# Local attention in a two-block fp32 kernel: GpSimd forms the high half of the gated output itself

## The chip, the cores and the metric

The kernel runs on one core of a Trainium2 chip. The metric is the device time of one execution in microseconds; lower is better. Engines are named as in the profile: PE (TensorE), DVE (VectorE), ACT (ScalarE), POOL (GpSimd), SP (SyncE, which issues DMAs here).

## The reference

Two transformer blocks over 512 tokens of width 1024, all in fp32. The part of the second block that matters here:

```python
q = rope(sw_q ...); k = rope(sw_k ...)
o_sw = sliding_window_sink_attention(q, k, sw_v, attn_sinks[l], valid)   # 16 query heads, 2 KV heads,
                                                                         # window 128, softmax with a sink
y_sb = (o_sb * jax.nn.silu(sb_z)) @ w_branch_sb[l]
y_sw = (o_sw * jax.nn.silu(sw_z)) @ w_branch_swa[l]                      # gate, then a 1024 x 1024 product
merged = jax.nn.sigmoid(g_sb) * y_sb + jax.nn.sigmoid(g_sw) * y_sw
h = h + merged @ w_out[l]
```

## The kernel before

Every fp32 matrix product is made of three PE passes. Each operand is split into a high part, rounded to the type fp32r that PE takes, and a low part, the remainder `value - high`, and PE adds high·high, low·high and high·low. So whatever feeds a product has to be split on the way.

The local attention works in 16 windows, `w = 4 n + u`: block `n` of 128 queries, and `u` one of four groups of four heads. Each engine runs its own instruction list, written by hand, and the lists meet in semaphores. For window `w`:

- PE: `window_scores` into PSUM; DVE: `window_max` (L1752) and `window_bias` (L1761, L1762, four numbers per partition); ACT: `window_exp` (L1081); DVE: `window_norm` (L1777 sum, L1778 reciprocal, which raises `inv_ready`).
- POOL: two products of the probabilities by the inverse sums (L619), each 128x512.
- PE: transposes (L2322); ACT copies them out of PSUM as the high part `pwt` (L905), DVE makes the low part (L1526); PE: `window_values` (L2336, L2338).
- ACT: `other_half` copies one half of the result (`other_part`, L905), DVE adds the other (`window_out`, L1743) into `yw`, a tile with two buffers, and raises `swo_read`.
- The gate: POOL multiplies `yw` by `gate_sw` in place (`window_gated`, L602), ACT copies the product to its place in `qw` as fp32r, the high part (`window_out_hi`, L905), and POOL subtracts that from `yw` and writes the low part beside it (`window_out_lo`, L610), which raises `ysw_ready`.

`qw` feeds the product with `w_branch_swa` after the last window; its first matmul waits for `ysw_ready` 16. `window_out(w)` on DVE waits for `ysw_ready` of window `w - 2`, since it writes the same buffer of `yw`.

The lists are skewed. In its turn `w` POOL makes the two L619 of window `w`, the gate product of window `w - 2` and the low part of window `w - 3`; DVE makes the norm of `w`, `window_out(w - 2)`, the low part of `pwt` of `w - 1`, and maximum and bias of `w + 2`; ACT makes the high part of `pwt` of `w - 1`, the exponentials of `w + 1`, `window_out_hi(w - 3)` and `other_half(w - 1)`. PE fills its list with single steps (three matmuls each) of the merge gate's product, one per turn and two in turns 4, 8 and 12. In turns 10 and 11 DVE also splits a quarter each of a weight slab (L1526, `wlo<-raw,whi`, 128x512). Turns are named by this `w`; a turn of POOL is counted from the start of its first L619.

Of the kernel before, what the change touches and what calls it, by code (L numbers as in the profile page):

```python
# [5 lines left out]
F32 = mybir.dt.float32  # L6
F32R = mybir.dt.float32r
ALU = mybir.AluOpType
# [4 lines left out]
P = 128  # L13
# [66 lines left out]
def insert_dim(ap, pos, n, step=0):  # L80

    dims = [list(d) for d in ap.ap]
    dims.insert(pos, [step, n])
    return bass.AP(ap.tensor, ap.offset, dims)
# [7 lines left out]
def build(nc, a, out):  # L92
    with ExitStack() as ctx:
        names = {}

        def sem(name):
            names[name] = ctx.enter_context(nc.semaphore(name))
            return names[name]
# [3 lines left out]
        def sb(name, shape, dt=F32, offset=None):  # L102
            size = 4 * int(np.prod(shape[1:]))
            size = (size + 31) // 32 * 32
            if offset is None:
                offset = at[0]
                at[0] += size
                assert at[0] <= nc.sbuf_usable_end, (name, at[0], nc.sbuf_usable_end)
            t = nc.alloc_sbuf_tensor_at(name, shape, dt, offset=offset)
            return t  # L110
# [94 lines left out]
        qw = sb("qw", [P, 16, SEQ], F32R)  # L205
# [7 lines left out]
        gate_sw = sb("gate_sw", [P, 8, SEQ])  # L213
        tokm = sb("tokm", [META, 3, 256])
        yw = sb("yw", [P, 2, 2, P], F32, r_sbias)
# [180 lines left out]
        yw_gated, yw_hi, ysw_ready = sem("yw_gated"), sem("yw_hi"), sem("ysw_ready")  # L396
# [123 lines left out]
        def _(pool):  # L520
# [77 lines left out]
            def window_gated(w):  # L598

                n, u = w // 4, w % 4  # L600
                pool.wait_ge(swo_read, w + 1)
                pool.tensor_tensor(yw[:, w % 2], yw[:, w % 2], gate_sw[:, 2 * u:2 * u + 2, n * P:n * P + P], ALU.mult)\  # L602
                    .then_inc(yw_gated, 1)

            def window_out_lo(w):

                n, u = w // 4, w % 4
                q = slice(n * P, n * P + P)
                pool.wait_ge(yw_hi, w + 1)
                pool.tensor_tensor(qw[:, 4 * u + 1:4 * u + 4:2, q], yw[:, w % 2], qw[:, 4 * u:4 * u + 4:2, q].bitcast(F32),  # L610
                                   ALU.subtract).then_inc(ysw_ready, 1)

            for w in range(16):

                nk = P + (META if w < 4 else P)
                pool.wait_ge(inv_ready, w + 1)
                for i in (2 * w, 2 * w + 1):
                    at_ = 128 + 4 * (i % 4)
                    pool.tensor_tensor(pw[:, i % 4, :, 0:nk], pw[:, i % 4, :, 0:nk],  # L619
                                       insert_dim(small2[:, at_:at_ + 2], 2, nk), ALU.mult).then_inc(pw_ready, 1)  # L620
                if w >= 2:
                    window_gated(w - 2)
                if w >= 3:
                    window_out_lo(w - 3)
            for w in (14, 15):
                window_gated(w)
                window_out_lo(w - 1)
            window_out_lo(15)
            for j in range(21, len(SLABS2)):
                if j in DVE_SLABS or j == 36:  # L630
                    continue
# [17 lines left out]
        def _(act):  # L649
# [63 lines left out]
            with act.Fori(0, DEPTH) as l:  # L713
# [36 lines left out]
                def transposed_hi(j):  # L750

                    act.wait_ge(tr_done, l * 47 + 10 + j + 1)
                    b = ps[:, T_BANK + j % 2, :]
                    if j < 4:
                        act.activation(qs[0:64, 2 * j, :], b[0:64], ACT.Copy).then_inc(thi_done, 1)
                        act.activation(qs[64:128, 2 * j + 1, :], b[64:128], ACT.Copy).then_inc(thi_done, 1)
                    else:
                        for g in range(2):
                            for half in range(2):
                                act.activation(khh[64 * half:64 * half + 64, g, :], b[64 * g:64 * g + 64],  # L760
                                               ACT.Copy).then_inc(thi_done, 1)
# [56 lines left out]
                for h in range(8):  # L818
# [6 lines left out]
                    for t in range(NT):  # L825
                        n = 4 * h + t
# [68 lines left out]
            def split2(j):  # L895
                s, n = j % RING, SLABS2[j][2]
                act.wait_ge(w_loaded[s], 16 * (DEPTH * SLABS // RING + j // RING + 1))
                act.wait_ge(unit_done, base + (UNITS_BY_SLAB2[j - 2] if j >= 2 else (UNITS_BY_SLAB[14] - UNITS, 0)[j]))
                act.activation(whi[s][:, 0:n, :], raw[s][:, 0:n, :], ACT.Copy).then_inc(whi_done, 1)  # L899
# [4 lines left out]
            def copy(o, i, scale=1.0):  # L904
                return act.activation(o, i, ACT.Copy, scale=scale)  # L905
# [165 lines left out]
            def window_exp(w):  # L1071
                nk = P + (META if w < 4 else P)
                by_i = lambda at_: small2[:, at_ + 8 * (w % 2):at_ + 8 * (w % 2) + 8].rearrange("p (i a) -> p i a", i=2)
                act.wait_ge(bias_ready, 2 * w + 2)
                if w >= 2:
                    act.wait_ge(tw_done, 10 + 2 * (w - 2) + 2)
                act.activation(by_i(64)[:, :, 2:4], by_i(96)[:, :, 0:2], ACT.Exp)
                for i in (2 * w, 2 * w + 1):
                    m = 4 * (i % 4)
                    for e in range(2):  # L1080
                        last = act.activation(pw[:, i % 4, e, 0:nk], ps[:, i % 4, 256 * e:256 * e + nk], ACT.Exp,  # L1081
                                              bias=small2[:, 32 + m + e:32 + m + e + 1],
                                              accum_out=small2[:, 64 + m + e:64 + m + e + 1])
                    last.then_inc(sw_exp, 1)
# [3 lines left out]
            def merge_tanh(i):  # L1088
                unit(54 + i)
                act.activation(tg[:, 2 * (i % 2) + i // 2, :], ps[:, 7, :], ACT.Tanh, scale=0.5).then_inc(g_tanh, 1)  # L1090

            def other_half(w):

                act.wait_ge(swo_done, w + 1)
                if w >= 2:
                    act.wait_ge(swo_read, w - 1)
                for e in range(2):
                    r, o = slice(64 * e, 64 * e + 64), slice(64 - 64 * e, 128 - 64 * e)
                    last = copy(other_part[r, w % 2], ps[o, 6, :].rearrange("p (c e n) -> p c e n", c=2, e=2)[:, :, e, :])
                last.then_inc(swo_copied, 1)  # L1100

            def window_out_hi(w):

                n, u = w // 4, w % 4
                act.wait_ge(yw_gated, w + 1)
                copy(qw[:, 4 * u:4 * u + 4:2, n * P:n * P + P], yw[:, w % 2]).then_inc(yw_hi, 1)

            for w in range(17):
                if w in (7, 13):
                    merge_tanh(w // 6)  # L1110
                if w:
                    transposed_hi(w - 1)
                if w < 15:
                    window_exp(w + 1)
                if w == 0:
                    merge_tanh(0)
                if w >= 3:
                    window_out_hi(w - 3)
                if w:
                    other_half(w - 1)  # L1120
                if w == 9:
                    split2(19)
            split2(20)
            window_out_hi(14)
            window_out_hi(15)
            merge_tanh(3)
            split2(21)
            split2(22)
# [1350 lines left out]
```

## Time and profile before

| | |
|---|---|
| time, median of 3 runs | 1007.69 us (1007.62 to 1007.7) |
| the profiled execution's own time | 1007.46 us |
| its span in the profile | 1005.4 us |
| PE busy | 979.6 us, 97% of the span |
| DVE busy | 624.1 us, 62% |
| ACT busy | 497.6 us, 49% |
| POOL busy | 260.5 us, 26% |
| granted PE clock | 0.998 of full speed |

The span is the stretch from the first to the last recorded instruction, and the profiled execution's own time is 2.06 us longer. The busy shares are means over stages with different limits: the windows of local attention lie between about 741 and 825 us of the span, and there the four engines are loaded quite differently from the whole.

### The profile page before, as it was taken

The numbers are of one execution on the slowest core, as the hardware profiler recorded it, in microseconds if no ns is written. First come the engines' busy times: TensorE is split into PE (matmuls) and PEld (weight loads), VectorE is DVE, ScalarE is ACT, GpSimd is POOL, SyncE is SP. The second block draws the span as 40 slices with busy tenths as digits, with TensorE's granted clock in tenths as the row PEclk, the third lists the DMA queues.
The fourth block names the chain that finished last, engine by engine and source line by source line (L and its number), as shares of the span: only waits on it lengthen the run. The fifth ranks groups of instructions, "written<-read, shape, count | busy, mean of one in ns | idle before, by whom it ended". The sixth has DMA issues, their size and how long they took to land.

```text
span 1005.4 us, 13802 instructions
## 1 busy us (share of the span) xinstructions
PE 979.6 (97%) x5015; PEld 824.8 (82%) x5015; DVE 624.1 (62%) x918; ACT 497.6 (49%) x887; POOL 260.5 (26%) x197
## 2 busy tenths in 40 slices
PE   6999999999999999999999999999999989999997
PEld 5988888888888888887888889888887768888886
DVE  4677678928777778928436586499558962213214
ACT  4435756525445656525357677423568972222122
POOL 2216200003216100003322031040326764223231
PEclk9999999999999999999999999999999999999999
DMA  8232201231432101241322020022320003323312
GB/s 288 96 120 76 77 22 43 84 128 55 137 116 85 63 22 43 84 154 34 123 84 84 1 70 21 37 84 84 107 81 2 30 14 105 105 84 105 116 52 84
DMA packets 66790, 80.44 MB, mean 80 GB/s; under 512 B 5520, under 2 KB 50704, under 8 KB 66720
## 3 DMA queue, kind: packets, MB, share of 16 engines
q1 hardware_dynamic: 64816, 76.64, 23.6%
q10 hardware_dynamic: 1904, 2.88, 0.9%
q8 instruction: 42, 0.69, 0.3%
q14 instruction: 28, 0.23, 0.1%
HBM read 77.42 MB, written 2.10 MB: 79 GB/s over the span
## 4 chain that ended last, share of the span: by engine, by line
PE 59%; issue 28%; DVE 6%; ACT 3%; POOL 2%; DMA 1%; POOLq 0%; ACTq 0%; DVEq 0%
PE ps L1850 16%; PE ps L1852 16%; PE ps L1851 16%; PE ps L1901 1%; PE ps L1903 1%; PE ps L1902 1%; DVE pwt L1526 1%; PE ps L2188 1%; DVE wr L1624 1%; PE ps L2336 1%; DMA x<-in_x 1%; POOL small L538 1%; DVE yw L1743 1%; PE ps L2338 1%; DVE qsb L1527 1%
## 5 line engine op out<-in xcount | busy, mean ns | idle before, releaser
L583 POOL TENSOR_TENSOR wlo<-raw,whi 128x2048 fp32r<-128x2048 f32 (+1 forms) x26 | 115.3, 4433 | 288.0 <-ACT whi L899 288.0
L1850 PE MATMUL ps<-whi,hhi 128*128 128x512 f32 (+1 forms) x320 | 116.6, 364 | 2.1 <-DVE hlo L1189 1.2
L1851 PE MATMUL ps<-wlo,hhi 128*128 128x512 f32 (+1 forms) x320 | 115.0, 359 | 0.0
L1852 PE MATMUL ps<-whi,hlo 128*128 128x512 f32 (+1 forms) x320 | 115.0, 359 | 0.0
L1850 PE MATMUL ps<-hhi,whi 128*128 128x512 f32 x288 | 113.2, 393 | 0.0
L1852 PE MATMUL ps<-hhi,wlo 128*128 128x512 f32 x288 | 112.2, 390 | 0.0
L1851 PE MATMUL ps<-hlo,whi 128*128 128x512 f32 x288 | 112.2, 390 | 0.0
L899 ACT ACTIVATE whi<-raw 128x2048 fp32r<-128x2048 f32 (+1 forms) x35 | 63.6, 1817 | 92.8 <-PE ps L1852 92.6
L665 ACT ACTIVATE whi<-raw 128x2048 fp32r<-128x2048 f32 (+1 forms) x29 | 52.2, 1799 | 72.4 <-PE ps L1852 72.4
L1198 DVE TENSOR_TENSOR wlo<-raw,whi 128x2048 fp32r<-128x2048 f32 (+1 forms) x29 | 63.5, 2190 | 39.4 <-ACT whi L665 38.1
L1901 PE MATMUL ps<-hhi,whi 128*128 128x512 f32 x192 | 76.8, 400 | 0.0
L1903 PE MATMUL ps<-hhi,wlo 128*128 128x512 f32 x192 | 75.1, 391 | 0.0
L1902 PE MATMUL ps<-hlo,whi 128*128 128x512 f32 x192 | 74.8, 390 | 0.0
L1526 DVE TENSOR_TENSOR wlo<-raw,whi 128x2048 fp32r<-128x2048 f32 (+1 forms) x10 | 19.9, 1990 | 88.4 <-ACT whi L899 88.4
L1850 PEld LDWEIGHTS ps<-whi,hhi 128*128 128x128 f32 x320 | 60.9, 190 | 12.1 <-issue 1.7
L1852 PEld LDWEIGHTS ps<-whi,hlo 128*128 128x128 f32 x320 | 60.8, 190 | 9.0
L1851 PEld LDWEIGHTS ps<-wlo,hhi 128*128 128x128 f32 x320 | 60.9, 190 | 8.5
L1852 PEld LDWEIGHTS ps<-hhi,wlo 128*128 128x128 f32 x288 | 54.0, 188 | 11.4
L1850 PEld LDWEIGHTS ps<-hhi,whi 128*128 128x128 f32 x288 | 54.1, 188 | 10.4
L1851 PEld LDWEIGHTS ps<-hlo,whi 128*128 128x128 f32 x288 | 54.1, 188 | 10.3
L569 POOL TENSOR_TENSOR small<-small 128x4 f32<-128x4 f32 x2 | 0.4, 202 | 226.9 <-ACT junk L860 226.9
L791 ACT ACTIVATE prob<-ps,small 128x512 f32<-128x512 f32 x64 | 43.5, 685 | 22.7 <-DVE small L1404 22.5
(310 smaller groups left out, 2336.4 us busy)
## 6 DMA issues: line engine op xcount, KB each, us to landing
raw<-in_w_in SPq DMA_DIRECT2D x42, 1024.0 KB, 5.3
raw<-in_w_out SPq DMA_DIRECT2D x12, 1024.0 KB, 5.0
raw<-in_w_in SPq DMA_DIRECT2D x10, 512.0 KB, 4.1
raw<-in_w_branch_swa SPq DMA_DIRECT2D x4, 1024.0 KB, 5.0
raw<-in_w_branch_sb SPq DMA_DIRECT2D x4, 512.0 KB, 3.5
x<-in_x ACTq DMA_DIRECT2D x3, 512.0 KB, 6.8
out<-x SPq DMA_DIRECT2D x3, 512.0 KB, 2.6
ws<-in_spatial_w SPq DMA_DIRECT2D x2, 512.0 KB, 6.8
```

The lines of the kernel that those rows point to most:

```text
L583: pool.tensor_tensor(wlo[s][:, 0:n, :], raw[s][:, 0:n, :], whi[s][:, 0:n, :].bitcast(F32), ALU.subtract).then_inc(slab_split, 1)
L665: act.activation(whi[s][:, :, 0:w], raw[s][:, :, 0:w], ACT.Copy).then_inc(whi_done, 1)
L791: act.activation(prob[:, t, :], ps[:, n % 3, :], ACT.Exp, bias=nmax[:, m:m + 1], accum_out=pair_sums(psum_e, h // 2)[:, m:m + 1]).then_inc ...
L899: act.activation(whi[s][:, 0:n, :], raw[s][:, 0:n, :], ACT.Copy).then_inc(whi_done, 1)
L1198: dve.tensor_tensor(wlo[s][:, :, 0:w], raw[s][:, :, 0:w], whi[s][:, :, 0:w].bitcast(F32), ALU.subtract).then_inc(slab_split, 1)
L1526: return dve.tensor_tensor(lo, src, hi.bitcast(F32), ALU.subtract)
L1850: pe.matmul(out_ap, lhsT=lhi(k), rhs=rhi(k), start=first and k == 0, stop=False, skip_group_check=True)
L1851: pe.matmul(out_ap, lhsT=lhi(k), rhs=rlo(k), start=False, stop=False, skip_group_check=True)
L1852: m = pe.matmul(out_ap, lhsT=llo(k), rhs=rhi(k), start=False, stop=last and k == n - 1, skip_group_check=True)
L1901: pe.matmul(ps[:, bank, :], lhsT=wh, rhs=hhi[:, k, :], start=k == 0, stop=False)
L1902: pe.matmul(ps[:, bank, :], lhsT=wh, rhs=hlo[:, k, :], start=False, stop=False)
L1903: m = pe.matmul(ps[:, bank, :], lhsT=wl, rhs=hhi[:, k, :], start=False, stop=k == KT - 1)
```

## The change

The high part in `qw` is no longer a copy that ACT makes of the gated product. POOL multiplies `yw` by the gate twice: once with the result rounded straight into `qw` (a new semaphore use: `yw_hi` is now raised by POOL), then once more in place in `yw`, and then subtracts. The three instructions of a window stand one behind the other in POOL's list, with a wait of POOL on its own semaphore ahead of the second and the third. The low part of a window is made in the same turn as its gate product, one turn earlier than before. ACT loses its 16 copies.

```diff
             def window_gated(w):
 
                 n, u = w // 4, w % 4
+                q = slice(n * P, n * P + P)
+                gate = gate_sw[:, 2 * u:2 * u + 2, q]
+                hi, lo = qw[:, 4 * u:4 * u + 4:2, q], qw[:, 4 * u + 1:4 * u + 4:2, q]
                 pool.wait_ge(swo_read, w + 1)
-                pool.tensor_tensor(yw[:, w % 2], yw[:, w % 2], gate_sw[:, 2 * u:2 * u + 2, n * P:n * P + P], ALU.mult)\
-                    .then_inc(yw_gated, 1)
-
-            def window_out_lo(w):
-
-                n, u = w // 4, w % 4
-                q = slice(n * P, n * P + P)
+                pool.tensor_tensor(hi, yw[:, w % 2], gate, ALU.mult).then_inc(yw_hi, 1)
                 pool.wait_ge(yw_hi, w + 1)
-                pool.tensor_tensor(qw[:, 4 * u + 1:4 * u + 4:2, q], yw[:, w % 2], qw[:, 4 * u:4 * u + 4:2, q].bitcast(F32),
-                                   ALU.subtract).then_inc(ysw_ready, 1)
+                pool.tensor_tensor(yw[:, w % 2], yw[:, w % 2], gate, ALU.mult).then_inc(yw_gated, 1)
+                pool.wait_ge(yw_gated, w + 1)
+                pool.tensor_tensor(lo, yw[:, w % 2], hi.bitcast(F32), ALU.subtract).then_inc(ysw_ready, 1)
...
                 if w >= 2:
                     window_gated(w - 2)
-                if w >= 3:
-                    window_out_lo(w - 3)
             for w in (14, 15):
                 window_gated(w)
-                window_out_lo(w - 1)
-            window_out_lo(15)
...
-            def window_out_hi(w):
-
-                n, u = w // 4, w % 4
-                act.wait_ge(yw_gated, w + 1)
-                copy(qw[:, 4 * u:4 * u + 4:2, n * P:n * P + P], yw[:, w % 2]).then_inc(yw_hi, 1)
-
...
-                if w >= 3:
-                    window_out_hi(w - 3)
                 if w:
                     other_half(w - 1)
...
-            window_out_hi(14)
-            window_out_hi(15)
```

POOL's list before, one turn of a window with full blocks and the start of the next (L619 the probabilities, L602 the gate product, L610 the low part):

```order
L619 TENSOR_TENSOR pw<-pw,small_95 128x512 [waits inv_ready]
L619 TENSOR_TENSOR pw<-pw,small_95 128x512
L602 TENSOR_TENSOR yw<-yw,gate_sw 128x256 [waits swo_read]
L610 TENSOR_TENSOR qw<-yw,qw 128x2x128 [waits yw_hi]
L619 TENSOR_TENSOR pw<-pw,small_95 128x512 [waits inv_ready]
```

And POOL's list at the same place in the changed kernel (L617 the probabilities, L605 the product rounded into `qw`, L607 the product in place, L609 the low part):

```order
L617 TENSOR_TENSOR pw<-pw,small_95 128x512 [waits inv_ready]
L617 TENSOR_TENSOR pw<-pw,small_95 128x512
L605 TENSOR_TENSOR qw<-yw,gate_sw 128x2x128 [waits swo_read]
L607 TENSOR_TENSOR yw<-yw,gate_sw 128x256 [waits yw_hi]
L609 TENSOR_TENSOR qw<-yw,qw 128x2x128 [waits yw_gated]
L617 TENSOR_TENSOR pw<-pw,small_95 128x512 [waits inv_ready]
```

A turn of POOL has five instructions where it had four, and its last two wait on the one just ahead of them.

ACT's list before, from the exponentials (L1081) of one turn to the copy of the transposed probabilities in the next:

```order
L1081 ACTIVATE pw,small_95<-ps,small_95 128x256 x4
L905 ACTIVATE qw<-yw 128x2x128 [waits yw_gated]
L905 ACTIVATE other_part<-ps 64x256 [waits swo_read,swo_done]
L905 ACTIVATE other_part<-ps 64x256
L905 ACTIVATE pwt<-ps 128x512 [waits swo_done,tw_done]
```

And in the changed kernel:

```order
L1075 ACTIVATE pw,small_95<-ps,small_95 128x256 x4
L899 ACTIVATE other_part<-ps 64x256 [waits swo_read,swo_done]
L899 ACTIVATE other_part<-ps 64x256
L899 ACTIVATE pwt<-ps 128x512 [waits swo_done,tw_done]
L899 ACTIVATE pwt<-ps 128x512 [waits tw_done]
```

The copy into `qw`, and with it ACT's wait for POOL, is gone; nothing else of ACT's list moves. The lists of PE, DVE and SP are the same but for their line numbers.

## Rows read from the trace of the kernel before

**Rows 1.** Busy time of all engines between 745 and 835 us: the sum

```profile
sum 90.00, PE 83.94 PEld 68.19 DVE 68.39 ACT 70.81 POOL 58.37; mean PE 4.66 PEld 3.79 DVE 3.80 ACT 3.93 POOL 3.24
```

**Rows 2.** Chain that ended last, turn 9: start us, us, engine, tile, line

```profile
789.08 1.30 DVE pwt L1526 x2
790.42 0.73 PE ps L2336 x2
791.15 0.48 PE ps L2338 x2
```

**Rows 3.** Timeline of PE, turns 7 and 8: start us, us, ..., [idle before]

```profile
781.46 0.74 PE L2336 MATMUL ps<-pwt,vw 128*128 128x512 f32 x2 [0.30 <-DVE pwt L1526]
...
786.17 0.62 PE L2336 MATMUL ps<-pwt,vw 128*128 128x512 f32 x2
```

**Rows 4.** Instructions that write tile yw or read it: ns min/median/max, first and last start

```profile
L905 ACT ACTIVATE qw<-yw x16: 394/442/455, 763.6 to 826.6; 128x256 fp32r<-128x256 f32 x16
```

**Rows 5.** Timeline of POOL, turn 9 and the start of turn 10

```profile
788.37 2.04 POOL L619 TENSOR_TENSOR pw<-pw,small 128x512 f32<-128x512 f32 x2 [0.65 <-DVE small L1778]
790.36 0.73 POOL L602 TENSOR_TENSOR yw<-yw,gate_sw 128x256 f32<-128x256 f32 x1
791.46 0.73 POOL L610 TENSOR_TENSOR qw<-yw,qw 128x256 fp32r<-128x256 f32 x1 [0.36 <-ACT qw L905]
792.84 2.04 POOL L619 TENSOR_TENSOR pw<-pw,small 128x512 f32<-128x512 f32 x2 [0.65 <-DVE small L1778]
```

**Rows 6.** Timeline of DVE, end of turn 9

```profile
790.29 1.28 DVE L1752 TENSOR_REDUCE small<-ps 128x2 f32<-128x512 f32 x2
791.60 0.61 DVE L1761 TENSOR_TENSOR small<-small 128x4 f32<-128x4 f32 x1
792.32 0.17 DVE L1762 TENSOR_TENSOR small<-small,sink 128x4 f32<-128x4 f32 x1
```

**Rows 7.** Timeline of POOL in the first block: the second product waits for the first

```profile
304.62 1.29 POOL L561 TENSOR_TENSOR t<-t,row_gain 128x512 f32<-128x512 f32 x1 [0.93 <-DVE t L1293]
305.99 1.29 POOL L563 TENSOR_TENSOR t<-t,row_gain 128x512 f32<-128x512 f32 x1
```

**Rows 8.** Timeline of DVE and POOL, end of turn 7

```profile
782.90 0.71 DVE L1762 TENSOR_TENSOR small<-small,sink 128x4 f32<-128x4 f32 x1
...
782.87 0.72 POOL L610 TENSOR_TENSOR qw<-yw,qw 128x256 fp32r<-128x256 f32 x1 [0.94 <-ACT qw L905]
783.98 2.04 POOL L619 TENSOR_TENSOR pw<-pw,small 128x512 f32<-128x512 f32 x2 [0.39 <-DVE small L1778]
```

**Rows 9.** Timeline of POOL: the starts of turns 5, 11, 12 and 14

```profile
769.91 2.04 POOL L619 TENSOR_TENSOR pw<-pw,small 128x512 f32<-128x512 f32 x2 [0.65 <-DVE small L1778]
...
798.16 2.04 POOL L619 TENSOR_TENSOR pw<-pw,small 128x512 f32<-128x512 f32 x2 [0.65 <-DVE small L1778]
...
802.78 2.04 POOL L619 TENSOR_TENSOR pw<-pw,small 128x512 f32<-128x512 f32 x2 [0.74 <-DVE small L1778]
...
811.84 2.04 POOL L619 TENSOR_TENSOR pw<-pw,small 128x512 f32<-128x512 f32 x2 [0.39 <-DVE small L1778]
```

**Rows 10.** Timelines of DVE and POOL: L1761 of turn 5, the slab's quarter in turn 11

```profile
773.58 0.72 DVE L1761 TENSOR_TENSOR small<-small 128x4 f32<-128x4 f32 x1
...
800.07 0.68 DVE L1526 TENSOR_TENSOR wlo<-raw,whi 128x512 fp32r<-128x512 f32 x1
...
801.98 0.17 DVE L1761 TENSOR_TENSOR small<-small 128x4 f32<-128x4 f32 x1
...
800.15 1.20 POOL L602 TENSOR_TENSOR yw<-yw,gate_sw 128x256 f32<-128x256 f32 x1
```

**Rows 11.** Timeline of all engines behind the last window

```profile
825.41 0.75 POOL L602 TENSOR_TENSOR yw<-yw,gate_sw 128x256 f32<-128x256 f32 x1 [2.83 <-DVE yw L1743]
...
826.41 2.29 DVE L1526 TENSOR_TENSOR wlo<-raw,whi 128x2048 fp32r<-128x2048 f32 x1 [1.08 <-ACT whi L899]
...
826.76 3.23 POOL L610 TENSOR_TENSOR qw<-yw,qw 128x256 fp32r<-128x256 f32 x2 [0.60 <-ACT qw L905]
...
830.09 0.47 PE L1850 MATMUL ps<-qw,whi 128*128 128x512 f32 x1 [1.00 <-issue]
```

## The prediction, made before the changed kernel ran

> **What bounds the kernel now.** I read the page first: PE is almost always busy, so a change away from PE moves the time only where PE waits. The chain that ended last is pure PE and issue for most of the span, but between 750 and 823 us it hops from engine to engine, so I went to that stretch. In the 90 us around it PE is idle for about 6 us, and DVE, ACT and POOL are each busy for 58 to 71 us [rows 1]: four engines close to full, in a ring. A piece of the chain shows the ring: DVE ends the low half of `pwt`, PE starts the values of the window 0.04 us later, and ACT, DVE and PE follow in the next turn [rows 2]. The timelines then show whose turn is longest. In turn 9 POOL's starts are 792.84 - 788.37 = 4.47 us apart [rows 5]; PE's values followed at 4.71 us where PE has two filler steps and did not wait (786.17 - 781.46) [rows 3], and at 790.42 - 786.17 = 4.25 us in the next turn, with one step [rows 2, 3]. So PE's own floor is 4.25 or less, and 4.71 in the turns with two steps.
>
> The reader is to see one more thing, which decides this case. DVE's L1761 works on four numbers per partition, yet it took 0.61 us in turn 9, and ended at 792.21, just behind POOL's L610, which ended at 792.19 [rows 5, 6]. Its neighbour L1762 took 0.17 us. In turn 7 it was L1762 that took 0.71 us: POOL's L610 had started 0.03 us ahead of it, and it ended 0.02 us behind that [rows 8]. L1752, which reads PSUM, ran beside POOL's product without a loss [rows 5, 6]. So DVE's instructions that read SBUF alone and POOL's products exclude each other, and whoever starts first is served whole. DVE then pays for each POOL product that lies across its four small instructions, and these stand between one turn of POOL and the next.
>
> **The change, part by part.**
>
> ACT loses 16 copies of 0.44 us [rows 4], and POOL no longer waits for them (0.36 us in turn 9 [rows 5]). By itself that is worth nothing: ACT is not the engine the values wait for in rows 2, and POOL idles 0.65 us behind the low part until DVE's reciprocal anyway [rows 5]. What hides it is DVE's part of the turn; if that were gone, the most it could give is in the last rival.
>
> POOL gets one more product and two waits on itself. The new product has the inputs of L602 and the output form of L610, both 0.73 us [rows 5], so 0.73. For a wait on the own semaphore the nearest row is a product that waits for the one before it: 305.99 - 304.62 = 1.37 us from start to start for a product of 1.29 us, so 0.08 us each [rows 7]. Bounds: zero if the wait were free, 0.08 as read; I take 0.08. Counted from the start of a turn of POOL, the gate comes at 790.36 - 788.37 = 1.99 [rows 5], and then:
>
> - product into `qw`: 1.99 to 2.72
> - product in place: 2.80 to 3.53
> - low part: 3.61 to 4.34 (in turn 9 before: 3.09 to 3.82)
>
> DVE gets to L1761 at 791.60 - 788.37 = 3.23 [rows 5, 6]. The product in place holds it until 3.55. L1762 follows 0.11 us behind its end (792.32 - 792.21 [rows 6]), at 3.66. But POOL's low part has started at 3.61. With a lead of 0.05 us it wins, as with the 0.03 us of rows 8, and L1762 ends at 4.36. The next turn of POOL starts 783.98 - 783.59 = 0.39 us behind a low part that held L1762 [rows 8]: 4.34 + 0.39 = 4.73 us per turn, where turn 9 had 4.47. Behind POOL's start are queued its two products for PE's transposes, and behind DVE's late norm `window_out` and the low half of `pwt`, on which PE's values wait [rows 2]. So the whole ring takes 4.73. The turns in which PE needs 4.71 take no more than that.
>
> The Trainium skill (Perfetto Trace Analysis, section GPSIMD Engine Instruction) says that a GpSimd span in a profile is unreliable, and that such instructions should be timed by the spacing of consecutive starts. With the spacing of products that do not wait, the two dependent products would end some 0.2 us earlier and the ring would hardly lengthen; rows 7 are such a spacing, with the wait in it, and they decide here.
>
> Now the sum, turns 5 to 13, which took 811.84 - 769.91 = 41.93 us before [rows 9]. Turn 4 comes out as before, since PE has two filler steps there; turn 5 starts 0.03 us later.
>
> - Turn 5: L1761 comes 773.58 - 769.91 = 3.67 late [rows 9, 10], because PE was late. It falls behind the low part, and then POOL's next start is 0.65 us behind that (792.84 - 792.19 [rows 5]): 4.34 + 0.65 = 4.99.
> - Turns 6, 7, 8, 9, 12, 13: 4.73 each, 28.38.
> - Turn 10 has a slab's quarter on DVE. It holds POOL's second product as it is held itself by the first; the low part ends at 4.67, L1761 waits for it, and with 0.65 the turn takes 5.32, which is what it took before (798.16 - 792.84 [rows 5, 9]).
> - Turn 11: the quarter starts 800.07 - 798.16 = 1.91 into the turn and ends at 2.59; POOL's first product, then under way, ends 0.60 us behind it as L602 did (801.35 - 800.75) [rows 9, 10], at 3.19. In place 3.27 to 4.00, low part 4.08 to 4.81. L1761 comes at 801.98 - 798.16 = 3.82 [rows 9, 10], ends at 4.02, L1762 at 4.13 loses to the low part: 4.81 + 0.39 = 5.20, where it took 802.78 - 798.16 = 4.62 [rows 9].
>
> Together 4.99 + 28.38 + 5.32 + 5.20 = 43.89, with the 0.03 us 1.99 us more than before. From turn 14 on DVE has no bias to make, and the ring runs as before.
>
> **The end of the stage.** PE stood still for 1.00 us before the first matmul on `qw` [rows 11]. Before, POOL's low parts of windows 14 and 15 (3.23 us together) were held by DVE's slab L1526, 826.41 to 828.70, and the second ended at 829.99. After, counted in the old times: product into `qw` 825.41 to 826.14, in place 826.22 to 826.95. That one is ahead of the slab and delays it by 0.5 us, to about 829.2. The low part waits for the slab and ends 0.6 behind it, at 829.8: 0.2 us less. The slab is needed by the same matmul, and is there by then.
>
> Sum: 1.99 - 0.2 = **+1.8 us**, against the profiled execution's 1007.46 us, which is 1009.3. The median of the runs is 0.23 above that execution, so the forecast is **1009.5 us**. The bounds of the self-wait and of the race give the rivals.
>
> **The rivals.**
>
> *DVE wins the race.* The lead of POOL is 0.05 us, the difference of two gaps read to 0.01. If L1762 gets in first, POOL's low part ends 0.6 us behind DVE's pair of small instructions, at about 4.49, and the next turn starts right there, at 4.44. Six turns of 4.44 save 1.7, turn 11 some 0.3: about -0.2 in all, 1007.5 us. Rows 8 speak against it. For it speaks only that in them POOL had been waiting for ACT, not for itself. The Trainium skill (SBUF, section SBUF: two separate sides) calls the port pair an exclusive lock held for the whole instruction, taken by whoever starts first; rows 8 agree, but no row shows a lead between 0 and 0.03 us.
>
> *L1761 itself falls behind the low part* (this one ends slower). If DVE comes 0.4 us later than 3.23 in most turns, as in turn 5, every turn takes 4.99: six times 0.26 and as much in turn 11, 1.8 us more, 1011.3 us. It needs DVE to wait for ACT or PE in a turn of 4.73; ACT has 0.44 us less to do and PE has slack in all but the turns with two steps, so I hold it for less likely. It decides from an arrival at 3.61.
>
> *No collision, and ACT's relief counts.* If POOL's products let the small instructions through, the ring falls to PE's pace: seven turns of 4.25 and two of 4.71, 39.2 us, 2.7 less than 41.93 [rows 2, 3, 9]. DVE's quarters in turns 10 and 11 give back up to 1.2. With the 0.2 of the end: 1.7 to 2.9 less, about 1005.4 us. Rows 6 and 8 speak plainly against it.
>
> **How the numbers follow.** A difference of 0.2%, 2.0 us, is about what a measurement of this kernel can tell from none. The forecast has 0.66, with a range of its own of 1008.5 to 1010.6, since a turn may come out 0.1 us off in either direction; its share above 1009.7 is 0.27. DVE wins: 0.14, nearly all within 0.2%. L1761 behind the low part: 0.13, slower. No collision: 0.07, of which 0.05 is faster by over 0.2%. Faster 0.06, the same 0.54, slower 0.40. The range of 1006.9 to 1011.2 takes in the forecast and the first rival and the lower part of the second.
>
> **What would show it.** In the changed kernel's profile: POOL's starts of L617 4.7 us apart in turns 6 to 9; DVE's L1762 (new line number) at 0.7 us in these turns and L1761 at about 0.3; ACT idle for longer ahead of `other_part`; PE waiting 0.4 to 0.7 us for `pwt` in one-step turns; PE's wait for `qw` at about 0.8 us; all of it worth some 2 us by the first matmul on `qw`, and nothing behind it. I am wrong if L1762 shows 0.17 us in these turns, if the low part starts more than 0.13 us behind the product before it, or if the product into `qw` is not 0.73 us long.

## The result, and the profile after

The changed kernel's median is 1009.35 us (1007.93 to 1010.64, 20 runs) against 1007.69 us (1005.57 to 1009.67, 20 runs) for the kernel before: a ratio of 1.0017, with a 95% interval of 1.0011 to 1.0023. It is slower by a hair, within the 0.2% that this measurement can tell. The 20 times of the changed kernel lie in two groups, nine from 1007.93 to 1009.02 us and nine from 1010.10 to 1010.64, with two between them, and its median falls into the gap. Its profiled execution took 1008.65 us, with a span of 1006.6 us where it was 1005.4.

The page of the changed kernel, busy time of each engine over the span:

```profile
PE 979.2 (97%) x5015; PEld 824.4 (82%) x5015; DVE 627.2 (62%) x918; ACT 493.0 (49%) x871; POOL 272.3 (27%) x213
```

PE's work is the same. POOL does 16 more instructions and 11.8 us more, ACT 16 fewer and 4.6 us less; DVE executes the same 918 instructions and is busy for 3.1 us more. That last difference is the one to follow. It lies in the window stage. These are two of DVE's groups between 745 and 835 us in the kernel before (line, tiles, count; busy us, mean ns; idle before):

```profile
L1762 DVE TENSOR_TENSOR small<-small,sink 128x4 f32<-128x4 f32 x14 | 3.4, 241 | 1.5
L1761 DVE TENSOR_TENSOR small<-small 128x4 f32<-128x4 f32 x14 | 5.1, 361 | 0.5
```

And these are DVE's small instructions there in the changed kernel:

```profile
L1746 DVE TENSOR_TENSOR small<-small,sink 128x4 f32<-128x4 f32 x14 | 6.1, 435 | 1.5
L1745 DVE TENSOR_TENSOR small<-small 128x4 f32<-128x4 f32 x14 | 4.5, 320 | 0.5
L1762 DVE RECIPROCAL small<-small 128x4 f32<-128x4 f32 x16 | 2.9, 178 | 0.7 <-DVE small L1761 0.2
```

L1745 and L1746 are the old L1761 and L1762 (the minimum and the addition of the sink), L1762 is now the reciprocal. The addition takes 435 ns in the mean where it took 241; unhindered it takes 160 to 170. The timelines of POOL and DVE show a turn, number 8, from 783.88 us, to be read beside [rows 5, 6, 8]:

```profile
783.88 2.04 POOL L617 TENSOR_TENSOR pw<-pw,small 128x512 f32<-128x512 f32 x2 [0.39 <-DVE small L1762]
785.87 0.73 POOL L605 TENSOR_TENSOR qw<-yw,gate_sw 128x256 fp32r<-128x256 f32 x1
786.69 0.73 POOL L607 TENSOR_TENSOR yw<-yw,gate_sw 128x256 f32<-128x256 f32 x1
787.50 0.73 POOL L609 TENSOR_TENSOR qw<-yw,qw 128x256 fp32r<-128x256 f32 x1
788.61 2.04 POOL L617 TENSOR_TENSOR pw<-pw,small 128x512 f32<-128x512 f32 x2 [0.38 <-DVE small L1762]
```

```profile
787.11 0.33 DVE L1745 TENSOR_TENSOR small<-small 128x4 f32<-128x4 f32 x1
787.54 0.71 DVE L1746 TENSOR_TENSOR small<-small,sink 128x4 f32<-128x4 f32 x1
788.17 0.15 DVE L1761 TENSOR_TENSOR small<-small 128x4 f32<-128x4 f32 x1
788.36 0.18 DVE L1762 RECIPROCAL small<-small 128x4 f32<-128x4 f32 x1
```

The minimum ends at 787.44, 0.02 us behind POOL's second product. The addition starts at 787.54, 0.04 us behind the start of POOL's low part, and ends at 788.25, 0.02 behind its end. Then come sum and reciprocal, and POOL's next turn 0.38 us behind its own low part. The turn is 4.73 us long. PE's values wait for the low half of `pwt`, and in three of the four turns shown that wait has grown with it. In turns 7, 9, 10 and 11 it was 0.30, 0.20, 0.77 and 0.67 us; now it is, in the timeline of PE:

```profile
781.19 0.74 PE L2320 MATMUL ps<-pwt,vw 128*128 128x512 f32 x2 [0.56 <-DVE pwt L1510]
...
790.67 0.72 PE L2320 MATMUL ps<-pwt,vw 128*128 128x512 f32 x2 [0.55 <-DVE pwt L1510]
...
795.61 0.73 PE L2320 MATMUL ps<-pwt,vw 128*128 128x512 f32 x2 [0.77 <-DVE pwt L1510]
...
800.73 0.73 PE L2320 MATMUL ps<-pwt,vw 128*128 128x512 f32 x2 [0.94 <-DVE pwt L1510]
```

Turns of POOL, us from start to start, read from its timelines (compare [rows 5, 9]):

| turn | 5 | 6 | 7 | 8 | 9 | 10 | 11 | 12 | 13 | sum |
|---|---|---|---|---|---|---|---|---|---|---|
| before | 5.01 | 4.27 | 4.79 | 4.39 | 4.47 | 5.32 | 4.62 | 4.22 | 4.84 | 41.93 |
| forecast | 4.99 | 4.73 | 4.73 | 4.73 | 4.73 | 5.32 | 5.20 | 4.73 | 4.73 | 43.89 |
| after | 5.01 | 4.74 | 4.74 | 4.73 | 4.74 | 5.32 | 5.20 | 4.74 | 4.74 | 43.96 |

The end of the stage, timeline of all engines (compare [rows 11]):

```profile
827.71 0.74 POOL L607 TENSOR_TENSOR yw<-yw,gate_sw 128x256 f32<-128x256 f32 x1
...
827.90 2.69 DVE L1510 TENSOR_TENSOR wlo<-raw,whi 128x2048 fp32r<-128x2048 f32 x1 [1.09 <-ACT whi L893]
828.53 2.65 POOL L609 TENSOR_TENSOR qw<-yw,qw 128x256 fp32r<-128x256 f32 x1
...
831.28 0.47 PE L1834 MATMUL ps<-qw,whi 128*128 128x512 f32 x1 [0.72 <-DVE wlo L1510]
```

POOL's product in place holds DVE's slab from 827.90 (it takes 2.69 us instead of 2.29), and the slab then holds POOL's low part, 2.65 us instead of 0.73. PE waits for 0.72 us where it waited for 1.00. The profile puts this wait down to the slab (done at 830.59); the low part was done at 831.18 and is the later one.

Two turns ahead of the table changed as well. POOL's turns 3 and 4 took 4.97 and 4.45 us before, and take 4.44 and 5.01 now. Before, a low part lay across DVE's minimum in turn 3 (L1761 took 0.68 us there); now one does so in turn 4 (L1745, 0.72 us). The two differences cancel, and turn 5 starts 0.03 us later, counted from turn 0.

From POOL's first start of turn 0 to this matmul the stage takes 831.28 - 745.37 = 85.91 us, before 830.09 - 745.92 = 84.17: **1.74 us more**. Behind the matmul there are 175.32 us, before 175.31. Ahead of the stage the changed kernel's execution happens to be 0.55 us ahead; the change does not reach there.

### The profile page after: what moved, and what is told of

Its sections match the earlier page's. It is cut to its first block, busy times and chain, and to the rows that moved or that the text cites. A ratio compares the mean times of both kernels' runs of the same rounds, so it can differ in the third digit from the quotient of the medians.

```text
span 1006.6 us, 13802 instructions
## 1 busy us (share of the span) xinstructions
PE 979.2 (97%) x5015; PEld 824.4 (82%) x5015; DVE 627.2 (62%) x918; ACT 493.0 (49%) x871; POOL 272.3 (27%) x213
## 4 chain that ended last, share of the span: by engine, by line
PE 58%; issue 28%; DVE 8%; ACT 2%; POOL 2%; DMA 1%; POOLq 0%; ACTq 0%; DVEq 0%
PE ps L1834 16%; PE ps L1836 15%; PE ps L1835 15%; DVE pwt L1510 2%; PE ps L1887 1%; PE ps L1885 1%; PE ps L1886 1%; PE ps L2172 1%; DVE yw L1727 1%; DVE small L1736 1%; DVE wr L1608 1%; DMA x<-in_x 1%; POOL small L538 1%; PE ps L2320 1%; DVE qsb L1511 1%
```

## The experiments

All times are medians, with the ratio to the kernel before on the same chip and its 95% interval. The kernel before had 1008.18, 1008.09 and 1008.21 us in the three groups. The ratio is not the quotient of the two medians, and can differ from it by 0.0006. The turns come from each kernel's own profile, and "the stage" is from turn 0 of POOL to the first matmul on `qw` (84.17 us before, 85.91 changed).

**Control: the changed kernel again.**

> The changed kernel again, beside the others of this group on one chip. Both theories: 1.7 us above the kernel before; turns of GpSimd 4.74 us long in turns 6 to 9, 12 and 13.

1010.06 us, 1.0020 (1.0010 to 1.0030): 1.9 us above. Turns of 4.74 and 4.75, nine of them 44.03 us. But the stage took 87.22 us, 1.3 more than in the first profile, and 1.2 of it lies behind the start of turn 14. The windows of PE from 810 us on show what differs there (us, PE busy, granted clock, DMA). The changed kernel's first profile:

```profile
810.00:815.00 5.00, 2.87 (x16) 1.00 0.00 0
815.00:820.00 5.00, 4.47 (x22) 1.00 0.00 0
```

The control:

```profile
810.00:815.00 5.00, 3.47 (x19) 1.00 0.00 2
815.00:820.00 5.00, 3.98 (x14) 0.66 0.00 0
```

In turn 14 PE stands still for 1.98 us (first profile) and 1.99 us (control). In the control the granted clock falls to 0.66 of full behind that, between its levels of 2.4 and 1.2 GHz in the mean of the stretch; in the first profile it does not. Such a fall at 815 us showed in one further profile, of the version with a tile of its own below.

**A pause on POOL: more work, at another moment.**

```diff
+        pause = sb("pause", [P, 8], F32)
...
                 pool.wait_ge(yw_gated, w + 1)
+                pool.memset(pause[:, 0:8], 0.0).then_inc(paused, 1)
+                pool.wait_ge(paused, w + 1)
                 pool.tensor_tensor(lo, yw[:, w % 2], hi.bitcast(F32), ALU.subtract).then_inc(ysw_ready, 1)
```

> The changed kernel with a small memset (8 numbers per partition) and a wait on it between GpSimd's product in place and its low part: more work on GpSimd, and the low part starts some 0.2 us later. Theory of the race (the lead of 0.05 us over DVE's second small product decides): DVE's second small product now comes first and takes 0.17 us instead of 0.7, turns of 4.45 to 4.5 us instead of 4.74, nine turns 1.5 to 2 us shorter, so about level with the kernel before (-0.3 to +0.3 us). Rival theory (GpSimd's own length of turn is the cost): each turn 0.2 to 0.3 us longer than 4.74, about 2 to 3 us slower than the changed kernel, 4 us above the kernel before.

1007.52 us, 0.9993 (0.9984 to 1.0002). Timelines of POOL and DVE, end of turn 8:

```profile
787.16 0.74 POOL L609 TENSOR_TENSOR yw<-yw,gate_sw 128x256 f32<-128x256 f32 x1
787.96 0.10 POOL L611 MEMSET pause<- 128x8 f32 x1
788.14 0.73 POOL L613 TENSOR_TENSOR qw<-yw,qw 128x256 fp32r<-128x256 f32 x1
788.84 2.04 POOL L621 TENSOR_TENSOR pw<-pw,small 128x512 f32<-128x512 f32 x2
```

```profile
787.38 0.54 DVE L1749 TENSOR_TENSOR small<-small 128x4 f32<-128x4 f32 x1
788.02 0.16 DVE L1750 TENSOR_TENSOR small<-small,sink 128x4 f32<-128x4 f32 x1
788.10 0.16 DVE L1765 TENSOR_TENSOR small<-small 128x4 f32<-128x4 f32 x1
788.29 0.18 DVE L1766 RECIPROCAL small<-small 128x4 f32<-128x4 f32 x1
```

The addition starts at 788.02, 0.12 us ahead of the low part, and takes 0.16 us. The turns fall to 4.48 to 4.50 us, now POOL's own chain with no idle at its end, and nine of them to 42.28. The low part starts 0.17 us later behind the second product, and the turn is 0.25 shorter: the order of two starts is the cost, not the amount of POOL's work. The rival is out. The stage took 83.87 us, 0.3 less than in the kernel before, at the edge of what was expected; the median lies 0.7 below, a little outside it.

**The second product in a tile of its own.**

```diff
+        yg = sb("yg", [P, 2, 2, P], F32)
...
+                pool.tensor_tensor(yg[:, w % 2], yw[:, w % 2], gate, ALU.mult).then_inc(yw_gated, 1)
                 pool.wait_ge(yw_hi, w + 1)
-                pool.tensor_tensor(yw[:, w % 2], yw[:, w % 2], gate, ALU.mult).then_inc(yw_gated, 1)
                 pool.wait_ge(yw_gated, w + 1)
-                pool.tensor_tensor(lo, yw[:, w % 2], hi.bitcast(F32), ALU.subtract).then_inc(ysw_ready, 1)
+                pool.tensor_tensor(lo, yg[:, w % 2], hi.bitcast(F32), ALU.subtract).then_inc(ysw_ready, 1)
```

> The changed kernel with the second product written to a tile of its own instead of in place, so that it needs no wait for the first: GpSimd's chain is 0.13 us shorter (0.08 of wait and 0.05 of overlap). Theory of the race: DVE's first small product is let go 0.13 us earlier, the second loses the race by the same 0.05 us, turns of 4.60 us, nine turns about 0.9 us shorter, 0.8 us above the kernel before. Rival (the self-wait costs nothing, something else sets the turn): no difference from the changed kernel.

1009.65 us, 1.0009 (1.0000 to 1.0018). The turns are 4.62 to 4.63 us, nine of them 43.27, 0.7 less than changed where 0.9 was expected: the size is about right, the way to it is not. Timelines of POOL and DVE, turn 7:

```profile
783.16 0.74 POOL L610 TENSOR_TENSOR qw<-yg,qw 128x256 fp32r<-128x256 f32 x1
784.22 2.04 POOL L618 TENSOR_TENSOR pw<-pw,small 128x512 f32<-128x512 f32 x2 [0.31 <-DVE small L1763]
```

```profile
783.14 0.17 DVE L1747 TENSOR_TENSOR small<-small,sink 128x4 f32<-128x4 f32 x1
783.22 0.70 DVE L1762 TENSOR_TENSOR small<-small 128x4 f32<-128x4 f32 x1
783.96 0.18 DVE L1763 RECIPROCAL small<-small 128x4 f32<-128x4 f32 x1
```

The addition started 0.02 us ahead of the low part and was not held, but the sum behind it, 0.06 us late, was, for the whole product. The collision moved by one instruction. Nor did the chain on POOL become 0.13 us shorter: the low part starts 1.57 us behind the product into `qw`, where it was 1.63, because it now starts 0.14 us behind the end of the second product (783.16 - 783.02) instead of 0.08. This execution had the clock at 0.66 at 815 us, too, and its stage took 86.26 us in spite of the shorter turns.

**The new product left out.**

```diff
                 pool.wait_ge(swo_read, w + 1)
-                pool.tensor_tensor(hi, yw[:, w % 2], gate, ALU.mult).then_inc(yw_hi, 1)
-                pool.wait_ge(yw_hi, w + 1)
                 pool.tensor_tensor(yw[:, w % 2], yw[:, w % 2], gate, ALU.mult).then_inc(yw_gated, 1)
```

> The changed kernel without the new product: the high part is not made at all (left out of the computation), the low part is taken against what lies in the tile. Theory of the race: GpSimd's low part ends at 3.53 us of its turn, holds DVE's first small product only, the second passes freely; the turns fall to the ring of PE, ACT and DVE, 4.25 to 4.3 us, 4.71 with two filler steps: 3.5 us less than the changed kernel, 1.8 us less than the kernel before. Rival theory (ACT's relief is what matters, or neither does): level with the kernel before.

1006.83 us, 0.9988 (0.9979 to 0.9997): 1.3 us below the kernel before, of the 1.8 expected. The addition never collides (0.16 or 0.17 us in all turns), and turns 6, 8 and 12 are 4.27, 4.26 and 4.20 us. But turn 10 takes 6.11 us instead of the 5.32 of both kernels: with the ring faster, DVE waits 0.71 us for ACT, which splits a slab there, and then its own quarter of a slab is held by POOL's low part (1.25 us). So nine turns are 41.88 us, level with the kernel before, and the gain against it is in turn 3 and at the end. Turns 3 and 4 both take 4.45 us, since no low part lies across DVE's minimum in either (before 4.97 and 4.45, changed 4.44 and 5.01). At the end, PE no longer waits for `qw`. The stage took 82.91 us, 1.26 less than before and 3.0 less than changed, of the 3.5 expected.

**ACT's work put back.**

```diff
+        spare = sb("spare", [P, 2, P], F32)
...
+                if w >= 3:
+                    if w > 3:
+                        act.wait_ge(spared, w - 3)
+                    copy(spare[:], gate_sw[:, 0:2, 0:P]).then_inc(spared, 1)
                 if w:
                     other_half(w - 1)
```

> The changed kernel with a copy of the size of the removed one put back in ACT's list at the same place (from the gate into a tile that nobody reads, so no wait for GpSimd): 14 copies of 0.44 us. My theory (ACT's relief is worth nothing in turns of 4.74 us): no difference from the changed kernel, within 0.2 us in the trace; turn 10, where ACT splits a slab, may be 0.1 to 0.2 us longer. Rival (the relief gives back part of the loss): 0.4 to 1 us slower than the changed kernel.

1009.65 us, 1.0019 (1.0010 to 1.0028). Nine turns of 43.97 us (43.96 without), the stage 85.94 (85.91). ACT's idle ahead of `other_part` between 770 and 815 us, groups of ACT, changed kernel and then this one:

```profile
L899 ACT ACTIVATE other_part<-ps 64x256 f32<-64x256 f32 x18 | 6.8, 378 | 7.1 <-PE ps L2322 7.0
```

```profile
L901 ACT ACTIVATE other_part<-ps 64x256 f32<-64x256 f32 x18 | 6.8, 378 | 4.4 <-PE ps L2328 4.1
```

The work freed on ACT had turned into waiting, and comes back without a trace in the time.

**The reciprocal ahead of the addition.** DVE's order in each turn becomes minimum, sum, reciprocal, addition.

```diff
+            def window_bias_norm(v, w):
...
+                count[0] += 1
+                dve.tensor_tensor(by_i(32), by_i(32), heads(small2[:, 160 + hp:164 + hp]), ALU.min).then_inc(dch, 1)
+                dve.wait_ge(sw_exp, 2 * w + 2)
+                link(dve.tensor_tensor(inv, sums[:, :, 0:2], sums[:, :, 2:4], ALU.add))
+                dve.reciprocal(inv, inv).then_inc(inv_ready, 1)
+                dve.tensor_tensor(by_i(96), by_i(32), heads(sink[:, hp:hp + 4]), ALU.add).then_inc(bias_ready, 2)
...
-                    window_bias(w + 2)
+                    window_bias_norm(w + 2, w + 1)
```

> The changed kernel with DVE's four small instructions in another order: minimum, sum, reciprocal, and only then the addition of the sink, so that the inverse no longer stands behind the instruction that loses the race. If the reciprocal (one SBUF input) can run beside a GpSimd product: the inverse is ready at 3.85 us of the turn, GpSimd's next turn starts behind its own low part at 4.29 us, turns of 4.29 (4.71 with two filler steps), 3.5 us less than the changed kernel, 1.8 us less than the kernel before. If the reciprocal is held like the others: turns of about 4.6 us, 1 us less than the changed kernel. Rival theory (a collision costs the same wherever it falls): no difference.

1005.66 us, 0.9979 (0.9970 to 0.9988): 2.4 us below the kernel before on this chip, and 4.0 below the version with ACT's work put back, its neighbour in this group. Timelines of POOL and DVE, end of turn 7:

```profile
781.15 0.73 POOL L609 TENSOR_TENSOR qw<-yw,qw 128x256 fp32r<-128x256 f32 x1
781.84 2.04 POOL L617 TENSOR_TENSOR pw<-pw,small 128x512 f32<-128x512 f32 x2
```

```profile
781.03 0.15 DVE L1776 TENSOR_TENSOR small<-small 128x4 f32<-128x4 f32 x1
781.22 0.18 DVE L1777 RECIPROCAL small<-small 128x4 f32<-128x4 f32 x1
781.32 0.59 DVE L1778 TENSOR_TENSOR small<-small,sink 128x4 f32<-128x4 f32 x1
```

The reciprocal runs inside POOL's low part in its usual 0.18 us; the addition is held (0.59), but POOL does not wait for it, and its next turn follows at once. Turns 7, 8, 12 and 13 are 4.31 to 4.34 us, near the 4.29 expected. Turns 5 and 6 stay at 4.76 and 4.74, and turn 9 at 4.69, because the minimum or the sum still meets the low part there. Nine turns: 41.40 us; the stage 83.11, 2.8 less than changed (3.5 were expected) and 1.06 less than before. So only some 1.1 of the 2.4 us against the kernel before are shown to come from the order. The rest lies outside the stage, which this execution also began 1.4 us sooner, and is not explained by the edit.

**The same order on the kernel before.**

> The kernel before with the same order of DVE's small instructions. Here the low part of GpSimd ends at 3.82 us and holds the minimum; sum and reciprocal follow at once: turns of 4.2 to 4.3 us, set by the ring of PE, ACT and DVE: 1.5 to 2 us less than the kernel before. If collisions do not set the turns: no difference.

1007.37 us, 0.9990 (0.9981 to 0.9999); nine turns 41.18 us, the stage 83.48, 0.7 less. The expectation of 1.5 to 2 us was more than twice too high. POOL's next turn does start sooner behind the low part, 0.38 us instead of 0.65, but in this kernel the low part waits for ACT's copy, and that comes later into the turn: in turn 9 the low part starts 3.35 us behind the start of the turn instead of 3.09, and the turn takes 4.47 us as before.

**Both together.**

> Both together on the changed kernel: the other order on DVE, and the second product in a tile of its own. GpSimd's chain is 4.16 us long, below the ring's 4.25: turns of 4.25 to 4.3 us, the same as or up to 0.3 us less than with the order alone; 2 us less than the kernel before.

1006.29 us, 0.9981 (0.9972 to 0.9990), the same as with the order alone within the intervals. Turns 8, 9 and 12 are 4.26, 4.30 and 4.26 us, as expected, but turn 10 takes 5.72, and turns 5 to 7 and 13 take 4.62 to 4.72. Nine turns are 42.03 us and the stage 83.38, so the profile shows no gain over the order alone.

**PE's filler steps dealt out otherwise**, on the changed kernel, on the kernel before and on the version with the other order. The list gives the steps done by the end of each turn; the last turns had 1, 3 and 3 and get 3, 2 and 2:

```diff
-GATE_STEPS = [1, 2, 3, 4, 6, 7, 8, 9, 11, 12, 13, 14, 16, 17, 18, 21, 24]
+GATE_STEPS = [1, 2, 3, 4, 6, 7, 8, 9, 11, 12, 13, 14, 16, 17, 20, 22, 24]
```

> The changed kernel with PE's filler steps of the last three turns dealt out otherwise: 3, 2 and 2 in turns 14, 15 and 16 instead of 1, 3 and 3 (the sum of 24 steps by turn 16 is kept). In the control's profile PE stood idle for 1.99 us in turn 14 and its granted clock was 0.66 of full in the 5 us from 815 us on; in the changed kernel's own profile it idled 1.98 us and the clock stayed full; its 20 runs lie in two groups, around 1008.6 and 1010.3 us. Theory (the upper group is the runs in which the clock falls there): PE's idle in turn 14 falls to about 0.6 us, no clock below full at 815 us, the upper group vanishes, the median is 1008.6 to 1009.2 us, 0.9 to 1.5 us above the kernel before; GpSimd's turns stay at 4.74. Rival (the groups come from the start of the kernel, where the clock differs from run to run): the two groups stay, median 1009.4.

> The kernel before with the same dealing of PE's filler steps. Its runs lie in one group, and its profile shows no clock below full at 815 us. Theory: no difference from the kernel before, within 0.3 us. Rival (moving work of PE ahead saves time by itself): 0.5 us or more faster.

> The version with DVE's other order (reciprocal ahead of the addition of the sink) on the changed kernel, with the same dealing of PE's filler steps. That version's runs spread from 1004.7 to 1007.6 us. Theory: the spread's upper part is the clock, and goes; median 1005.2 us, 2.9 us below the kernel before. Rival: spread and median as without it, 1005.7 us.

On the changed kernel 1009.15 us, 1.0007 (0.9998 to 1.0016); on the kernel before 1007.60 us, 0.9995 (0.9986 to 1.0004); on the other order 1006.16 us, 0.9983 (0.9974 to 0.9992), against 0.9979 without. On the changed kernel PE's wait in turn 14 fell from 1.98 to 0.61 us, but waits of 0.82 and 0.81 us came up in turns 15 and 16; nine turns stayed at 43.96, the stage took 85.95 us (85.91 without), and the clock was full. The runs still lie in two groups, around 1008.1 and 1009.6 us (1008.6 and 1010.3 without this edit). The interval of the first ratio overlaps that of the control, so a gain is not shown. The two sets of runs were not made side by side, and the groups did not vanish, as the theory had asked; a clock that falls in turn 14 is not shown to be their cause. On the kernel before, the interval takes in both no difference and the 0.5 us of the rival. On the other order the result is the rival's: 2.0 us below the kernel before instead of 2.9, with the spread left.

## Why the prediction was right

The forecast was 1009.5 us, measured were 1009.35. The mechanism is borne out in the turns and by the pause; that the totals meet within 0.15 us is partly luck, since the median lies in the gap between two groups around 1008.6 and 1010.3 us, and the profiled execution took 1008.65 us for a forecast of 1009.3.

- *The race.* POOL's low part was to start 0.05 us ahead of DVE's addition; it started 0.04 or 0.05 us ahead and won in each turn that the forecast named. The pause shows that this order is the cause, since turning it round by a low part 0.17 us later took the loss away.
- *The turn.* 4.73 us forecast, 4.73 to 4.74 measured; the three special turns within 0.02 us; the nine together 0.07 us off. Turn 0 to the first matmul on `qw` came out at +1.74 us for a forecast of +1.8.
- *Turn 4.* The forecast had it as before because of PE's two filler steps, with turn 5 0.03 us later, a figure that it gave without a row. The start of turn 5 was right, the reason was not: turn 4 grew by 0.56 us from a collision and turn 3 shrank by 0.53 from one that went away. This cancelling was luck. With neither collision, in the version without the new product, turn 4 took 4.45 us, so PE's steps do not keep it at 5.01.
- *The self-wait.* 0.08 us read from the first block, 0.08 to 0.09 measured (786.69 - 786.60 = 0.09).
- *The end.* 0.2 us less forecast, 0.28 measured.
- *ACT's relief.* Nothing forecast; nothing found when its work was put back.
- *The Trainium skill's rule* that GpSimd spans should be timed by starts (Perfetto Trace Analysis, section GPSIMD Engine Instruction): the spacing of dependent starts, taken from the trace with its wait, held (0.81 us forecast, 0.81 to 0.82 in turn 8). The lock on the port pair, which the Trainium skill (SBUF — State Buffer, section SBUF: two separate sides) gives to whoever starts first, held for DVE's instructions with two SBUF inputs. The prediction's own reading, that all of DVE's instructions that read SBUF alone are excluded, was too wide: the reciprocal, with one SBUF input, was not held. No sum of the forecast hung on that.

Two things were not in it, and the close agreement of the totals owes something to them. The start of the kernel varies: turn 0 began between 744.53 and 747.93 us in the thirteen profiles, more than the change is worth, and in the changed kernel's own profile 0.55 us sooner. And in some executions the clock falls behind PE's wait in turn 14, as in the control, worth 1.2 us there. The forecast named neither. How much of the measured +1.66 us is the turns and how much these two is shown for the profiled executions only: the first profile has 1.74 us more in the stage and starts it 0.55 sooner, 1.19 in all.

One step of a rival was wrong. Had DVE won, POOL's low part was to end 0.6 us late and the turn to take 4.44. In the pause version DVE won and the low part was not held at all (0.73 us); the turn was 4.49 from POOL's own chain. With the tile of its own DVE's addition ran 0.15 us into the low part, which took 0.74. I had taken the 0.6 from a DVE instruction of 512 columns; over the thirteen profiles one of four numbers per partition cost a POOL product at most 0.04 us (0.77 instead of 0.73). The last rival's nine turns were too short as well: it had 39.2 us and up to 1.2 for the slabs, with no collision on the addition they took 41.88, and no version came below 41.18.

## What to carry to other kernels

In this kernel an instruction moved to GpSimd was paid for by the small VectorE instruction with two SBUF inputs that fell on it. Look for tiny instructions with long durations that end with a GpSimd product, and count whether each stands ahead of a semaphore on the ring. Where they cannot be kept apart, put the result that others wait for ahead of the one that will be held; here that order of four instructions turned a loss of 0.2% into a gain of 0.2% against the kernel before, of which the profile places about half in the stage. Relieving ACT, which only waited, was worth nothing here, and adding work to POOL even helped, since it moved a start.

## What was not expected of the hardware

A few hundredths of a microsecond decide about 0.55 us. In the thirteen profiles no DVE instruction of 128x4 with two SBUF inputs was held that started 0.01 to 0.14 us ahead of one of POOL's products on `yw`, and each that started 0.03 to 0.12 us behind one was (0.63 to 0.72 us). Between 0 and 0.02 us behind, both came up: 0.73 us in turn 5 of the changed kernel, 0.16 in turn 9 of the version with both edits. What decides there stays open. VectorE's reciprocal of 128x4, one SBUF input, ran in 0.18 us in the middle of GpSimd products that held additions of the same size for 0.48 to 0.61 us. PE's granted clock fell to 0.66 of full in a stretch of 5 us behind a wait of 1.99 us in one execution and stayed full behind one of 1.98 us in another of the same kernel; what decides between them stays open.
